# Middle block of a three-branch, S5 and GLA kernel: more convolution taps early, variance sums inside ev_a.1, and y kept in chunk order

## The reference, cut to what matters

```python
p = rms_norm(x, norm_pre) @ ev_w_in      # a_in, a_z2, b_val, b_gate, b_z2: 1024 columns each
y = gelu(s5_layer(a_in))                 # 64 groups of 16 channels, 64 complex states each
y = y * sigmoid(y @ s5_w_glu + b_glu) * silu(a_z2)
h = conv(b_val * sigmoid(b_gate))        # causal, depthwise, 31 taps, and a bias
h = silu(layer_norm(h)) @ w_pw + b_pw
h = h * silu(b_z2)
x = x + rms_norm(concat(y, h) @ ev_w_out, norm_post)
```

## Time and profile before

| what | value |
| --- | --- |
| median of 3 runs | 1795.4 us (1794.92 to 1797.2) |
| profiled execution | 1794.97 us, span 1793.2 us |
| TensorE matmul busy | 1667.4 us, 93% |
| VectorE busy | 928.9 us, 52% |
| ScalarE busy | 666.2 us, 37% |
| GpSimd busy | 203.4 us, 11% |
| memory read and written | 190.94 MB and 14.68 MB, 115 GB/s over the span |

### The profile page before, as it was taken

The page is one execution under the profiler, slowest core; times in us unless marked ns, Lnnn a source line. Parts: engine busy times, 40 slices in busy tenths (PEclk is TensorE's granted clock), DMA queues, the critical chain, the costliest instruction groups (busy, mean ns, idle before and its releaser), DMA issues.

```text
span 1793.2 us, 20084 instructions
## 1 busy us (share of the span) xinstructions
PE 1667.4 (93%) x7876; PEld 1359.2 (76%) x7876; DVE 928.9 (52%) x1293; ACT 666.2 (37%) x920; POOL 203.4 (11%) x234
## 2 busy tenths in 40 slices
PE   6999989999999999989999989475989999999997
PEld 5887878878888888879988777354877778687775
DVE  4265264552246234558889937912464344453446
ACT  5333332223212223354544465216344334342442
POOL 4980000000000000031222202101000000000000
PEclk9999999999999999999999989797999999999999
DMA  8455433333333332257789838217422223132211
GB/s 245 127 155 152 131 94 94 94 117 106 99 101 94 94 98 102 95 211 161 145 216 195 162 132 187 48 62 184 131 60 64 78 71 105 48 104 60 82 48 59
DMA packets 151227, 206.75 MB, mean 115 GB/s; under 512 B 51963, under 2 KB 74987, under 8 KB 150123
## 3 DMA queue, kind: packets, MB, share of 16 engines
q1 hardware_dynamic: 131915, 173.62, 31.4%
q0 software_dynamic: 17568, 29.89, 10.2%
q10 hardware_dynamic: 1664, 2.13, 0.4%
HBM read 190.94 MB, written 14.68 MB: 115 GB/s over the span
## 4 chain that ended last, share of the span: by engine, by line
PE 89%; DVE 4%; ACT 3%; issue 2%; DMA 1%; SPq 0%; ACTq 0%; DVEq 0%
PE PS L2010 76%; PE PS L1988 2%; PE PS L2225 1%; PE PS L2277 1%; PE PS L2295 1%; PE PS L2164 1%; PE PS L2286 1%; PE PS L2131 1%; ACT XN L900 1%; DVE V L1391 1%; DMA WR<-in_conv_w_pw_dram 1%; PE PS L2194 1%; PE PS L2305 0%; DVE WL L1309 0%; PE PS L2179 0%
## 5 line engine op out<-in xcount | busy, mean ns | idle before, releaser
L2010 PE MATMUL PS<-HH,WH 128*128 128x512 f32 x1216 | 478.4, 393 | 10.5 <-issue 5.4
L2010 PE MATMUL PS<-HL,WH 128*128 128x512 f32 x1216 | 475.3, 391 | 0.0
L2010 PE MATMUL PS<-HH,WL 128*128 128x512 f32 x1216 | 475.2, 391 | 0.0
L893 ACT ACTIVATE WH<-WR 128x1024 fp32r<-128x1024 f32 x200 | 211.6, 1060 | 688.6 <-PE PS L2010 641.4
L1309 DVE TENSOR_TENSOR WL<-WR,WH 128x1024 fp32r<-128x1024 f32 x144 | 185.4, 1294 | 420.5 <-ACT WH L893 420.4
L2010 PEld LDWEIGHTS PS<-HH,WH 128*128 128x128 f32 x1216 | 229.7, 189 | 60.5 <-issue 10.8
L2010 PEld LDWEIGHTS PS<-HL,WH 128*128 128x128 f32 x1216 | 229.8, 189 | 48.2 <-issue 1.0
L2010 PEld LDWEIGHTS PS<-HH,WL 128*128 128x128 f32 x1216 | 229.4, 189 | 47.8
L2010 PE MATMUL PS<-WH,HH 128*128 128x512 f32 x384 | 153.2, 399 | 9.1 <-DVE WL L1309 4.2
L2010 PE MATMUL PS<-YH,WH 128*128 128x512 f32 x320 | 126.7, 396 | 36.0 <-DVE YL L1346 31.3
L1685 DVE SCALAR_TENSOR_TENSOR TMP<-CP,PRM,TMP 128x512 f32<-128x512 f32 x232 | 154.9, 740 | 0.0
(11 more groups left out here) (328 smaller groups left out, 1965.0 us busy)
## 6 DMA issues: line engine op xcount, KB each, us to landing
WR<-in_w_in_dram SPq DMA_DIRECT2D x96, 512.0 KB, 3.7
WR<-in_od_w_in_dram SPq DMA_DIRECT2D x32, 512.0 KB, 3.9
WR<-in_ev_w_in_dram SPq DMA_DIRECT2D x24, 512.0 KB, 3.9
WL<-in_ev_w_in_dram POOLq DMA_DIRECT2D x24, 512.0 KB, 7.5
WR<-in_ev_w_in_dram SPq DMA_DIRECT2D x32, 256.0 KB, 3.2
WR<-in_ev_w_out_dram SPq DMA_DIRECT2D x16, 512.0 KB, 4.2
WR<-in_od_w_in_dram SPq DMA_DIRECT2D x32, 256.0 KB, 3.4
WR<-in_od_w_out_dram SPq DMA_DIRECT2D x16, 512.0 KB, 3.8
```

Source lines behind the costliest of these rows:

```text
L893: act.activation(WH[:, n % RING, :, :], WR[:, n % RING, :, :], ACT.Copy).then_inc(w_hi, 1)
L2010: mm = pe.matmul(out_banks[m], st, mv, start=(kt == 0 and i == 0), stop=(kt == 2 * per - 1 and i == 2))
```

## The change

- VectorE's taps: 92 (not 78) ahead of the recurrence, 58 (not 36) behind it; none between the first four parts of y and one after each of the second four; 20, then 10 ahead of the gate of glu.0; 10, the low parts, 10 more, and the gate of glu.1; then low parts and the remaining 16.
- ScalarE: one `split()` moves from ahead of the drain of b_z2.0 to behind it. y_t has one drain there (YH, not reordered) and YA is no longer copied: VectorE makes the low part and the gated product from PSUM. AZ (the silu of a_z2) is written in chunk order, with a stride.
- TensorE: ev_a.1 is cut. Its first chunk, then the variance sums, then its other three chunks. ScalarE takes the square root after the split of pw's first chunk, then does SiLU and splits by turns, and drains ev_a.1 last.
- VectorE interleaves the normalisation with the low parts, two slices apart.
- y, and so ev_a's output rows, x1 and the final output, are in chunk order: row c of tile t is token 4c + t. So ev_b, the transposes u2_t (in their PSUM output) and the output products of the GLA heads use `strided`, and x1 and the output move with `by_chunk`.

```diff
-    _add(f"y_t.{_i}", side=4, a=4)
+    _add(f"y_t.{_i}", side=4, d=4)
-_add("var", a=1)
+_add("var")
+        def by_chunk(dram):
+            return dram.rearrange("(c t) d -> c t d", t=T4)
+        def chunked(v):
+            return v.rearrange("p (t c) -> p c t", t=T4)
             sp.wait_ge(sq_used, KT)
-            sp.dma_start(X1[:, :, :], tokens(d_x1)).then_inc(x1_in, 16)
-            sp.wait_ge(ya_gated, 8)
+            sp.dma_start(X1[:, :, :], by_chunk(d_x1)).then_inc(x1_in, 16)
+            sp.wait_ge(banks_dve, dve_after("y_t.1"))
...
-                sp.dma_start(tokens(out[0])[:, t, :], YO2[:, t, :]).then_inc(fin_out, 16)
+                sp.dma_start(by_chunk(out[0])[:, t, :], YO2[:, t, :]).then_inc(fin_out, 16)
...
-            evac("a_z2.0", [AZ[:, m, :] for m in range(4)], ACT.Silu)
+            evac("a_z2.0", [chunked(AZ[:, m, :]) for m in range(4)], ACT.Silu)
             split()
-            evac("a_z2.1", [AZ[:, 4 + m, :] for m in range(4)], ACT.Silu)
-            split()
+            evac("a_z2.1", [chunked(AZ[:, 4 + m, :]) for m in range(4)], ACT.Silu)
             split()
             act.wait_ge(carried, 1)
             evac("b_z2.0", [BZ[:, m, :] for m in range(4)], ACT.Silu)
+            split()
...
-                    src = bank(f"y_t.{i}", m).rearrange("p (t c) -> p t c", t=T4)
-                    act.activation(YH[:, 4 * i + m, :].rearrange("p (c t) -> p t c", t=T4), src, ACT.Copy).then_inc(y_hi, 1)
-                    act.activation(YA[:, 4 * i + m, :].rearrange("p (c t) -> p t c", t=T4), src, ACT.Copy).then_inc(banks_act, 1)
+                    act.activation(YH[:, 4 * i + m, :], bank(f"y_t.{i}", m), ACT.Copy).then_inc(y_hi, 1)
...
-            split()
+            split(1)
+            act.wait_ge(sq_used, KT)
+            act.activation(RS[:, :], bank("var", 0), ACT.Sqrt, bias=EPS[:, 0:1]).then_inc(var_read, 1)
+            split(1)
+            z_silu(range(4))
+            split(1)
+            z_silu(range(4, KT))
+            split(1)
             evac("ev_a.1", [YO[:, m, NC:D] for m in range(4)], ACT.Copy)
...
-            convolve(78)
+            convolve(92)
...
-            convolve(36)
+            convolve(58)
...
-                    dve.tensor_tensor(YL[:, kt, :], YA[:, kt, :], YH[:, kt, :].bitcast(F32), ALU.subtract).then_inc(y_lo, 1)
-                    convolve(1)
-                    dve.tensor_tensor(YA[:, kt, :], YA[:, kt, :], AZ[:, kt, :], ALU.mult).then_inc(ya_gated, 1)
+                    dve.tensor_tensor(YL[:, kt, :], bank(f"y_t.{i}", m), YH[:, kt, :].bitcast(F32), ALU.subtract).then_inc(y_lo, 1)
+                    dve.tensor_tensor(YA[:, kt, :], bank(f"y_t.{i}", m), AZ[:, kt, :], ALU.mult).then_inc(banks_dve, 1)
+                    convolve(i)
...
-            convolve(16)
+            convolve(20)
             for u in range(2):
                 if u:
-                    convolve(21)
+                    convolve(10)
                     h_low(3, lambda kt: YA[:, kt, :], range(4))
-                dve.wait_ge(ya_gated, 4 * u + 4)
+                    convolve(10)
+                dve.wait_ge(banks_dve, dve_after(f"y_t.{u}"))
...
-            section("ev_a", H, ready(h_lo, 3), rows=True, units=(1,))
+            free("ev_a.1")
+            ev_banks = [bank("ev_a.1", m) for m in range(4)]
+            unit(chunks_before("ev_a.1"), ev_banks, H, lambda kt: None, True, tile, chunks=(0,))
             free("var")
...
+            unit(chunks_before("ev_a.1"), ev_banks, H, lambda kt: None, True, tile, chunks=(1, 2, 3))
             section("pw", Y, ready(y_lo, 4))
-            section("ev_b", H, ready(h_lo, 4), rows=True, by_tile=True)
-            turn_tokens("u2_t", XN2, xn2)
+            section("ev_b", H, ready(h_lo, 4), rows=True, tok=strided, by_tile=True)
+            turn_tokens("u2_t", XN2, xn2, strided)
```

More of the change, by code:

```diff
@@ L404, in three_branch_s5_gla_kernel @@
         powers, carried, fixed = sem("powers"), sem("carried"), sem("fixed")
-        ya_gated, z_cent, z_sq, z_norm, z_act, ones_in = (sem(n) for n in (
-            "ya_gated", "z_cent", "z_sq", "z_norm", "z_act", "ones_in"))
+        var_read, z_cent, z_sq, z_norm, z_act, ones_in = (sem(n) for n in (
+            "var_read", "z_cent", "z_sq", "z_norm", "z_act", "ones_in"))
         sq3, std3, x2_done, sq4, std4, xn2 = (sem(n) for n in ("sq3", "std3", "x2_done", "sq4", "std4", "xn2"))
@@ L927, in evac @@
                     extra = {k: v(m) for k, v in kw.items()}
-                    act.activation(o, bank(job, m), func, **extra).then_inc(inc, 1)
+                    src = bank(job, m)
+                    if job.startswith("a_z2"):
+                        src = src.rearrange("p (c t) -> p c t", t=T4)
+                    act.activation(o, src, func, **extra).then_inc(inc, 1)
             def value_gate(i):
@@ L1170, in _, with z_silu @@
                 act.activation(SQ[:, kt, :], CP[:, kt, CPAD:], ACT.Square).then_inc(z_sq, 1)
-            split()
-            evac("ev_a.1", [YO[:, m, NC:D] for m in range(4)], ACT.Copy)
[L1173 to L1180, removed]
+            split(1)
+            act.wait_ge(sq_used, KT)
+            act.activation(RS[:, :], bank("var", 0), ACT.Sqrt, bias=EPS[:, 0:1]).then_inc(var_read, 1)
+            def z_silu(kts):
+                for kt in kts:
+                    act.wait_ge(z_norm, kt + 1)
+                    act.activation(CP[:, kt, CPAD:], CP[:, kt, CPAD:], ACT.Silu, scale=col("ln_g2", kt),
+                                   bias=col("ln_b2", kt)).then_inc(z_act, 1)
+                    act.wait_ge(z_act, kt + 1)
+                    act.activation(YH[:, kt, :], CP[:, kt, CPAD:], ACT.Copy).then_inc(y_hi, 1)
+            split(1)
[3 more added lines that the diff above has]
+            split(1)
+            evac("ev_a.1", [YO[:, m, NC:D] for m in range(4)], ACT.Copy)
             split()
@@ L1714, in _ @@
                     kt = 4 * i + m
-                    dve.wait_ge(banks_act, act_after(f"y_t.{i}", m + 1))
                     dve.wait_ge(y_hi, 24 + kt + 1)
-                    dve.tensor_tensor(YL[:, kt, :], YA[:, kt, :], YH[:, kt, :].bitcast(F32), ALU.subtract).then_inc(y_lo, 1)
-                    convolve(1)
-                    dve.tensor_tensor(YA[:, kt, :], YA[:, kt, :], AZ[:, kt, :], ALU.mult).then_inc(ya_gated, 1)
+                    dve.tensor_tensor(YL[:, kt, :], bank(f"y_t.{i}", m), YH[:, kt, :].bitcast(F32), ALU.subtract).then_inc(y_lo, 1)
+                    dve.tensor_tensor(YA[:, kt, :], bank(f"y_t.{i}", m), AZ[:, kt, :], ALU.mult).then_inc(banks_dve, 1)
+                    convolve(i)
             dve.memset(ONES[:, :], 1.0 / D).then_inc(ones_in, 1)
             seq.wait()
-            convolve(16)
+            convolve(20)
             for u in range(2):
                 if u:
-                    convolve(21)
+                    convolve(10)
                     h_low(3, lambda kt: YA[:, kt, :], range(4))
-                dve.wait_ge(ya_gated, 4 * u + 4)
+                    convolve(10)
+                dve.wait_ge(banks_dve, dve_after(f"y_t.{u}"))
                 times_tmp([(f"glu.{u}", m, YA[:, 4 * u + m, :]) for m in range(4)], GLUV)
@@ L1741, in _ @@
             dve.memset(BNA[:, 0, 0:1], 0.0).then_inc(banks_dve, 1)
-            dve.wait_ge(banks_act, act_after("var"))
+            dve.wait_ge(var_read, 1)
             seq.inc(dve.reciprocal(RS[:, :], RS[:, :]))
@@ L1745, in _ @@
             dve.wait_ge(z_sq, 8)
-            for kt in range(KT):
-                dve.tensor_tensor(CP[:, kt, CPAD:], CP[:, kt, CPAD:], RS[:, :], ALU.mult).then_inc(z_norm, 1)
-            y_low(4, lambda kt: CP[:, kt, CPAD:], range(8))
+            for kt in range(KT + 2):
+                if kt < KT:
+                    dve.tensor_tensor(CP[:, kt, CPAD:], CP[:, kt, CPAD:], RS[:, :], ALU.mult).then_inc(z_norm, 1)
+                if kt >= 2:
+                    y_low(4, lambda kt: CP[:, kt, CPAD:], [kt - 2])
             for u in range(2):
@@ L1761, in _ @@
             split(3)
-            dve.wait_ge(ya_gated, 8)
+            dve.wait_ge(banks_dve, dve_after("y_t.1"))
             dve.memset(LWH[:, :, :].bitcast(F32), 0.0).then_inc(lw_zero, 1)
@@ L2042, in turn, with turn_tokens @@
                     mm.then_inc(side_done, 1)
-            def turn_tokens(job, x, s):
+            def turn_tokens(job, x, s, tok=tile):
                 for i in range(2):
@@ L2050, in turn_tokens @@
                     for kt in range(KT):
-                        mm = pe.transpose(bank(f"{job}.{kt // 4}", kt % 4)[:, t * P:(t + 1) * P], x[:, t, kt * P:(kt + 1) * P],
+                        mm = pe.transpose(tok(bank(f"{job}.{kt // 4}", kt % 4), t), x[:, t, kt * P:(kt + 1) * P],
                                           ident[:, :])
@@ L2224, in step @@
                     for i, (wi, ai) in enumerate(halves):
-                        mm = pe.matmul((B, A)[u][t], tile(acts(kt)[ai], t), (WH, WL)[wi][:, 2 * u + kt // 2, kt % 2, :],
```

(5 more changed lines are left out.)

## The result

The changed kernel takes 1765.74 us (median of 4 runs, 1765.6 to 1766.61) against 1795.56 (4 runs, 1794.92 to 1797.2): the ratio is 0.9827, interval 0.9814 to 0.9841. That is 29.8 us faster. The forecast was 1752.6 with a range from 1746 to 1760, so the direction was right and the size, 43 us, was not: 13 us of it are missing. The profiled execution has a span of 1764.0 us.

A forecast was written before the change was run, and what follows sets the result against it. TensorE was taken as the bound, busy 93% of the span, with time to come from its waits, half clock or pace. Net gains of 42.8 us from 1794.97, plus 0.43, gave 1752.6 us; range 1746 to 1760.

The forecast's parts named there:

- Taps: VectorE's convolution taps: 14 more ahead of the recurrence, 22 more behind it, leaving 16 after glu instead of 61.
- To the mean: From glu to the mean: it starts at g + 74.0 instead of g + 96.9, gain 22.9; at full clock, 2.3 more.
- strided tiles: ev_b and output units: strided stationary tiles cost 8.3 ns a product, 4.2 us over 504 products.
- The split: Ahead of the recurrence's output products: moved behind b_z2.0's drain, their second half starts at 1042.1, gain 4.8 us.
- y in chunk order: Between the output products and glu: contiguous high parts, VectorE gating from PSUM; path 6.3 instead of 8.4 us, gain 2.1.
- the clock ahead of glu: TensorE's idle time before glu shrinks to about 2.6 us, so glu avoids half clock, gain 2.9 us.
- the cut of ev_a.1: Variance sums after one chunk of ev_a.1: mean end to variance end 12.35 instead of 28.7 us, gain 16.35.
- Variance end to pw: Stretch ahead of pw: ScalarE's last-placed drain of ev_a.1 makes it 35.4 instead of 31.25 us, loss 4.15.
- The first (the clock falls ahead of glu): Rival at glu: the 2.9 us stays, 1755.5; 1 to 2 more if also at second half or mean; chance 0.20.
- The third: Rival ahead of pw: the chunk-order x1 read uses few DMA engines, 60 us more on two, 1812; chance 0.02.
- The second: Rival: ordered lists slip; table 1 us later, ev_a waits 2, x1 and weights 3 later, 1758.6; chance 0.12.
- The fourth: Rival at the variance: it waits for squares or its bank and runs where it did, 16.35 lost, 1765; chance 0.04.

## Why the prediction was wrong, point by point

- **Step "Taps" and step "To the mean": this is the step that failed, by its size.** "16 taps are left after glu instead of 61" and "the last 16 taps end at g + 73.9" rest on a misread indentation. 26 are left; ten times 0.664 is 6.6 us, and the hole ahead of the mean is 5.89 us, not 0.5. The run with the ten taps put in closes the hole and is 8.0 us faster, which shows it; so does the run with the taps alone, whose time came out as its corrected count said.
- **The same step, the clock.** "With a hole of 0.5 the mean runs at full clock" was right for such a hole: 6.87 us in three runs without one. With 5.89 it is 10.05. So the miscount cost 9.2 us in all, over a third more than the taps themselves.
- **"it then starts at half clock as before, no difference" and strided tiles.** The last stretch, 4.4 us longer by forecast, became 6.6 longer. The stride is worth what was priced where it can be read by itself. The other 2 us lie in products after waits that the change didn't touch. I had priced such stretches at no change, but whether they run at 1.2 GHz differs from kernel to kernel, by 1.5 us for one and the same unit (17.94 to 19.45). Why is open; no run held the order of work fixed and moved only this.
- **The first block** was 1.45 us longer in the profiled execution, with unchanged work. The same mark lies at 385.05, 386.50, 386.07, 384.91 and 387.32 in five profiles. A sum against one execution carries this error, and the range had no term for it.
- **The split, y in chunk order, the clock ahead of glu, the cut of ev_a.1: right where they were priced.** Measured 4.2, 2.1, 2.6 and 16.35 for 4.8, 2.1, 2.9 and 16.35. The table landed at 1043.86 and was late next, as said. The clock stayed up through a hole of 2.64 us. What had no term is ev_a.0 behind it: it was priced at its 23.63 of before, and took 24.79. It took 23.63 in the two kernels whose glu took 46.4 (before, and the taps alone), and 24.6 to 24.8 in all others, whose glu took 43.8 to 45.4; whether the one causes the other is not shown.
- **Variance end to pw: right**, 34.7 for 35.4, for the reason given. That this loss was avoidable, the prediction did not say: it priced the list as it stood.
- **Signs.** Of the signs of being wrong that the prediction named, one showed: the last stretch is longer by more than 6 us (6.6). The recurrence is later than 901, at 902.66, but 1.45 of these 1.6 us are the first block's.
- **Rivals.** The first (the clock falls ahead of glu) is out, but its rider, that the clock falls at the mean, came true behind the 5.89 us hole. The third (x1 on few engines; it landed after 7.8 us) is out. The second was about lists that slip by a microsecond or two; none of its three did, on the measured rows: apart from the 1.45 us of the first block the table was 0.3 late, ev_a.0 has no wait inside it, and the weights landed 9.7 us behind the variance sums (10.5 forecast). The fourth is out by the 12.35 us. None of the four was "the code does less of this than I read".

## What to carry to other kernels

When a list of work is redistributed, add up the pieces: 28 + 92 + 58 + 4 + 20 + 10 + 10 + 26 = 248, and what is left at the end is what the next engine waits for. Hold one hole on TensorE as costing its length plus the half clock that can follow it, here 3.2 us for 5.9 and nothing for 2.64. And a drain that frees banks belongs in its engine's list where the work that needs them would start, not behind everything else that happens to be ready; here three reorderings of existing instructions were worth 27.7 us on top of the change's 29.8.

## What the runs showed of the hardware

- A stationary operand read with a step of four fp32 values loads in 309 ns instead of 188, and a product then costs 0.235 us instead of 0.2267: most of the slower load is hidden under a product of 512 columns.
- ScalarE's drain of AZ with a step of 128 values in SBUF takes 1.17 us for 512 values, the contiguous one 0.60; the y drain with a step of four took 1.11 before.
- Transposes of 128 columns that write PSUM with a step of four values are as fast as contiguous ones: 273 ns is the median record of both.
- The clock stayed at 1.00 through a hole of 2.64 us and was at 0.50 behind holes of 3.5 and 5.9 us; the mean behind the latter took 10.05 us, without a hole 6.87.
